# Hyena convolution at half-integer frequencies with an even/odd split, and a minimum in banded attention

## The reference

```python
def _bidir_long_conv(u, h_fwd, h_bwd, skip):
    l = u.shape[1]
    n = 2 * l
    filt = jnp.concatenate([h_fwd, jnp.zeros_like(h_fwd[:1]), h_bwd[:0:-1]], axis=0)
    uf = jnp.fft.rfft(u.astype(jnp.float32), n=n, axis=1)
    ff = jnp.fft.rfft(filt, n=n, axis=0)
    y = jnp.fft.irfft(uf * ff[None], n=n, axis=1)[:, :l]
    return (y + u.astype(jnp.float32) * skip.astype(jnp.float32)).astype(u.dtype)
```

## Time and profile before

| | |
|---|---|
| median of 3 runs | 2266.3 us (2265.16 to 2270.39) |
| profiled execution, its own time | 2263.19 us |
| its span, mean granted clock | 2261.4 us, 0.989 |
| busy: PE, PEld, DVE, ACT, POOL | 96%, 78%, 64%, 39%, 10% of the span |
| layer 1, last tile's end to w_out | 805.3 to 893.15 us from the span's start |
| layer 2, attention | 1394.8 to 1484.3 us |

### The profile page before, as it was taken

One profiled execution on the slowest core, in us unless ns is written; L12 is line 12 of the kernel. 1 busy time (PEld: TensorE's weight loads), 2 busy tenths in 40 slices (PEclk: granted clock), 3 DMA queues, 4 the chain that ended last, 5 costly groups with the idle time before them and its releaser, 6 DMA issues.

```text
span 2261.4 us, 28637 instructions
## 1 busy us (share of the span) xinstructions
PE 2161.1 (96%) x11616; PEld 1754.8 (78%) x11616; DVE 1439.3 (64%) x2224; ACT 885.7 (39%) x1337; POOL 216.7 (10%) x253
## 2 busy tenths in 40 slices
PE   6999999999999988999999999999999999998998
PEld 4767888888787756788888786478888878868996
DVE  3426668778666443658788745965778775655554
ACT  3335533332253411443332244845333223455543
POOL 0000011110010025011110002100111100100110
PEclk9999999999999989999999999999999999999999
DMA  9650345556532210335556522022455563214554
GB/s 312 201 172 1 112 130 168 158 158 205 205 119 74 84 37 10 112 112 161 165 157 215 195 86 84 2 84 94 148 168 159 189 202 126 94 38 140 187 186 140
DMA packets 224744, 304.96 MB, mean 135 GB/s; under 512 B 6738, under 2 KB 153243, under 8 KB 224486
## 3 DMA queue, kind: packets, MB, share of 16 engines
q1 hardware_dynamic: 220541, 290.11, 39.5%
q0 software_dynamic: 3664, 12.87, 1.7%
q10 hardware_dynamic: 409, 0.16, 0.0%
HBM read 302.00 MB, written 1.11 MB: 134 GB/s over the span
## 4 chain that ended last, share of the span: by engine, by line
PE 78%; DVE 11%; ACT 5%; DMA 4%; issue 2%; POOL 0%; SPq 0%; ACTq 0%; DVEq 0%; POOLq 0%
PE lo L648 16%; PE lo L650 16%; PE lo L649 16%; PE lo L714 4%; PE lo L715 3%; PE lo L716 3%; DVE w_lo L1471 2%; ACT w_hi L1126 2%; DMA w_raw<-in_ffn_w_down 2%; PE hi L714 2%; PE hi L715 2%; PE hi L716 2%; PE lo L1041 2%; PE hi L1054 1%; PE modp L614 1%
## 5 line engine op out<-in xcount | busy, mean ns | idle before, releaser
L648 PE MATMUL lo<-u_hi,w_hi 128*128 128x512 f32 (+1 forms) x2016 | 717.6, 356 | 5.5 <-DVE w_lo L1471 4.5
L649 PE MATMUL lo<-u_lo,w_hi 128*128 128x512 f32 (+1 forms) x2016 | 704.8, 350 | 0.0
L650 PE MATMUL lo<-u_hi,w_lo 128*128 128x512 f32 (+1 forms) x2016 | 704.3, 349 | 0.0
L1471 DVE TENSOR_TENSOR w_lo<-w_raw,w_hi 128x2048 fp32r<-128x2048 f32 (+1 forms) x182 | 406.7, 2235 | 343.1 <-ACT w_hi L1126 341.9
L1126 ACT ACTIVATE w_hi<-w_raw 128x2048 fp32r<-128x2048 f32 (+1 forms) x182 | 339.7, 1867 | 484.0 <-DMA w_raw<-in_ffn_w_down 262.5
L648 PEld LDWEIGHTS lo<-u_hi,w_hi 128*128 128x128 f32 x2016 | 382.5, 190 | 69.8 <-issue 17.5
L650 PEld LDWEIGHTS lo<-u_hi,w_lo 128*128 128x128 f32 x2016 | 382.4, 190 | 50.0
L649 PEld LDWEIGHTS lo<-u_lo,w_hi 128*128 128x128 f32 x2016 | 382.6, 190 | 49.1 <-issue 1.2
L1488 DVE SCALAR_TENSOR_TENSOR mod_acc<-mod_raw,silu_c,mod_acc 128x512 f32<-128x512 f32 x504 | 394.5, 848 | 7.3 <-DMA mod_raw<-in_mod_w 7.3
L2035 POOL TENSOR_TENSOR mid_lo<-conv,mid_hi 128x512 fp32r<-128x512 f32 (+1 forms) x88 | 117.8, 1358 | 1054.8 <-ACT mid_hi L1450 1054.8
L714 PE MATMUL lo<-w_hi,mid_hi 128*128 128x512 f32 x374 | 147.6, 395 | 4.9 <-DVE u_raw L1569 3.1
(11 more groups left out here) (314 smaller groups left out, 2741.6 us busy)
## 6 DMA issues: line engine op xcount, KB each, us to landing
w_raw<-in_ffn_w_up SPq DMA_DIRECT2D x88, 1024.0 KB, 5.1
mod_raw<-in_mod_w SPq DMA_DIRECT2D x144, 512.0 KB, 4.0
w_raw<-in_ffn_w_down SPq DMA_DIRECT2D x40, 1024.0 KB, 5.1
mod_unit<-in_mod_w SPq DMA_DIRECT2D x24, 1024.0 KB, 6.7
w_raw<-in_a_w_qkv SPq DMA_DIRECT2D x12, 1024.0 KB, 5.5
w_raw<-in_b_w_in SPq DMA_DIRECT2D x12, 1024.0 KB, 5.1
w_raw<-in_a_w_out SPq DMA_DIRECT2D x8, 1024.0 KB, 5.1
w_raw<-in_ffn_w_down SPq DMA_DIRECT2D x8, 512.0 KB, 3.6
```

The lines of the kernel that those rows point to most:

```text
L648: mm(o, h3[:, k, c], x, start=(first and k == 0), stop=False)
L649: mm(o, h3[:, k, c], y, start=False, stop=False)
L650: ins = mm(o, l3[:, k, c], x, start=False, stop=(last and k == nr - 1))
L1471: tt(WL[:, n % 3, 0:words], RAW[:, n % 3, 0:words], WH[:, n % 3, 0:words].bitcast(F32), ALU.subtract).then_inc(lo_ready, 1)
```

## The change

**Transform.** Frequencies k + 1/2 take the place of 0 to 256, so that no frequency is special and four blocks of filter_spec remain. Tokens are taken as 128 even and 128 odd ones (stationary operands with a step of two columns, rows of k_decay and k_dft reordered). For each of real and imaginary part one matmul on the even and one on the odd tokens (E and O) give frequency k as E + O and 255 - k as E - O (O - E for the imaginary part): ACT copies O out of PSUM (`odd_part`), DVE adds and subtracts (`butterflies`). A filter pair is two matmuls instead of four, a window's forward four instead of eight.

**Order.** Window 0 (turn, forward, butterflies, products, and POOL's y) and the turn of window 1 move into the tiles 8 to 11. `products` reads the spectrum from SBUF and writes two of its four products over it; y reads these. ACT makes both copies of a turn.

**Attention.** The fused operation of `peak` multiplies by -scale and takes the minimum, started from the negated sink; `negate` goes away for layer 2. `sinkn`, the negated sink, is made once; exp runs with scale -1.

```diff
+    pos = np.arange(SEQ, dtype=np.float64)[:, None]
+    th = 2 * np.pi * ((pos * (2 * np.arange(SEQ)[None, :] + 1)) % (2 * NFREQ)) / (2 * NFREQ)
+    out["k_dft"] = np.concatenate([np.cos(th[:, :P]), -np.sin(th[:, :P])], axis=1)[by_parity].astype(f)
+    order = np.concatenate([np.arange(P), SEQ - 1 - np.arange(P)])
+    ang = th.T[order]
+    out["k_idft"] = (2.0 / NFREQ * np.concatenate([np.cos(ang), -np.sin(ang)], axis=0)).astype(f)
...
         XFIRST = [FIRST["down" if k % 2 else "out", k // 2] for k in range(2 * DEPTH)]
+        def f_bank(w, j):
+            return bank[j + 4 if w == 0 else j]
+        def spectrum(w, j):
+            return XS[:, j, :] if w % 2 == 0 else (CV, SQ)[j % 2][:, j // 2, :]
         def x_bank(h, b):
...
                         ps = slice(FW * d, FW * d + FW)
-                        last = mm(bank[6 + d], FA[ps, 1, tt * P:(tt + 1) * P], W4[ps, hf * 512:(hf + 1) * 512],
+                        last = mm(bank[6 + d], FA[ps, 1, tt:SEQ:2], W4[ps, hf * 512:(hf + 1) * 512],
                                   start=True, stop=True)
                     last.then_inc(f_mm, 1)
                 else:
-                    pe.wait_ge(f_h, 4)
-                    for x in range(2 * (t - 7), 2 * (t - 7) + 2):
-                        j, hf = divmod(x, 2)
-                        if x >= 2:
-                            pe.wait_ge(f_sev, x - 1)
-                        src = HD if j in (2, 3) else HS
-                        blk = (0, 1, 5, 3, 4)[j]
-                        for kt in range(2):
-                            last = mm(bank[6 + x % 2], DF[:, kt, blk * P:(blk + 1) * P], src[:, kt, hf * 512:(hf + 1) * 512],
-                                      start=(kt == 0), stop=(kt == 1))
+                    for pair in ((0, 1), (2,), (3,), (), ())[t - 7]:
+                        hf, im = divmod(pair, 2)
+                        pe.wait_ge(f_h, 4)
+                        if pair >= 2:
+                            pe.wait_ge(f_sev, 2 if pair == 2 else 6)
+                        for e in range(2):
+                            last = mm(bank[(4 if pair == 1 else 6) + e], DF[:, e, im * P:(im + 1) * P],
+                                      (HD if im else HS)[:, e, hf * 512:(hf + 1) * 512], start=True, stop=True)
                         last.then_inc(f_spec, 1)
+            def turn_x1v(w):
+                hf, st = divmod(w, 2)
+                pe.wait_ge(z_conv, 2 * KT if hf == 0 else 3 * KT)
+                if w == 0:
+                    pe.wait_ge(f_sev, 4)
+                else:
+                    pe.wait_ge(c_vt, 2 * w)
+                if w == 1:
+                    pe.wait_ge(c_fly, 2)
+                for e in range(2):
+                    for c in range(4):
+                        last = nc.tensor.transpose(bank[4 + e][:, c * P:(c + 1) * P],
+                                                   XV[:, 4 * hf + c, st * SEQ + e:(st + 1) * SEQ:2], ident)
+                    last.then_inc(c_turned, 1)
+            def forward(w, im):
+                pe.wait_ge(c_vt, 2 * w + 2)
+                if w == 0 and im:
+                    pe.wait_ge(f_sev, 8)
+                if w == 1 and not im:
+                    pe.wait_ge(*released(PAIR0["in", 1] + 10))
+                if w == 1 and im:
+                    pe.wait_ge(z_evac, 3 * KT)
+                if w >= 2:
+                    pe.wait_ge(c_fly, 4 * w - 2 + 2 * im)
+                for e in range(2):
+                    last = mm(f_bank(w, 2 * im + e), DF[:, e, im * P:(im + 1) * P], VX[:, w % 2, e, :], start=True, stop=True)
+                last.then_inc(c_fwd, 1)
             def long_conv():
...
                 def inverse(w):
                     pe.wait_ge(c_y, 4 * (w + 1))
                     if w == 0:
                         pe.wait_ge(tab_in, TAB_AT[1] + 16)
...
                     else:
                         pe.wait_ge(c_skip, 4 * w)
...
+                def spectra(w):
+                    forward(w, 0)
+                    forward(w, 1)
+                spectra(1)
+                inverse(0)
+                turn_x1v(2)
+                spectra(2)
+                turn_x1v(3)
+                inverse(1)
+                spectra(3)
+                inverse(2)
+                inverse(3)
...
                         tile(n0 + t, q0 + t, TOK, UH, UL, True, True)
                         filter_stage(t)
+                        if t == 8:
+                            turn_x1v(0)
+                        if t == 9:
+                            forward(0, 0)
+                        if t == 10:
+                            forward(0, 1)
+                            turn_x1v(1)
                     long_conv()
                     arrive = lambda k: pe.wait_ge(c_lo, 8 * (k // 4 + 1))
-                    free = lambda b: ((c_prod, 32),)
+                    free = lambda b: ((c_fly, 16),)
                 else:
...
@@ -1267,7 +1282,7 @@
                     if A:
                         src, dst, sc = s_bank(x), p[:, 0:TOK], q_scale[:, 0, 4 * h + t:4 * h + t + 1]
                     else:
-                        src, dst, sc = p[:, 0:TOK + 1], p[:, 0:TOK + 1], 1.0
+                        src, dst, sc = p[:, 0:TOK + 1], p[:, 0:TOK + 1], -1.0
                     last = f(dst, src, ACT.Exp, scale=sc, bias=sl[:, 1, 0:1], accum_out=sl[:, 2, 0:1])
...
                         w = FW if t < 2 else 2 * FW
                         f(FA[0:w, (t + 1) % 2, :], FT[0:w, 0, :], ACT.Sin).then_inc(f_sin, 1)
-                    elif t >= 7:
-                        for x in range(2 * (t - 7), 2 * (t - 7) + 2):
-                            j, hf = divmod(x, 2)
-                            act.wait_ge(f_spec, x + 1)
-                            f(BF[:, j, hf * 512:(hf + 1) * 512], bank[6 + x % 2], ACT.Copy).then_inc(f_sev, 1)
+                    for pair in {7: (0, 1), 8: (2,), 9: (3,)}.get(t, ()):
+                        hf, im = divmod(pair, 2)
+                        act.wait_ge(f_spec, pair + 1)
+                        f(BF[:, 2 * im + 1, hf * 512:(hf + 1) * 512], bank[(4 if pair == 1 else 6) + 1], ACT.Copy).then_inc(f_odd, 1)
+                    if t in (9, 10):
+                        odd_part(0, t - 9)
+                    if t in (8, 10):
+                        turned((t - 8) // 2)
+            def odd_part(w, im):
+                act.wait_ge(c_fwd, 2 * w + im + 1)
+                if w >= 2:
+                    act.wait_ge(c_y, 4 * (w - 1))
+                f(spectrum(w, 2 * im + 1), f_bank(w, 2 * im + 1), ACT.Copy).then_inc(c_odd, 1)
+            def turned(w):
+                for e in range(2):
+                    act.wait_ge(c_turned, 2 * w + e + 1)
+                    if w >= 2:
+                        act.wait_ge(c_fwd, 2 * w - 2)
+                    f(VX[:, w % 2, e, :], bank[4 + e], ACT.Copy).then_inc(c_vt, 1)
             def long_conv():
-                def vt(w):
-                    act.wait_ge(c_turned, w + 1)
-                    if w >= 2:
-                        act.wait_ge(c_fwd, w - 1)
-                    f(VX[:, w % 2, 0, :], bank[4], ACT.Copy).then_inc(c_vt_act, 1)
                 def part(w):
                     hf, st = divmod(w, 2)
...
                     if t == 0:
                         dve.wait_ge(*((tab_in, TAB_AT[i]) if i else (start_in, 32)))
+                    if t + i == 0:
+                        ts(sinkn[:, :], sinkb[:, :], -1.0, None, ALU.mult)
                     for j in turned_in(i, t + 1):
                         rope(i, j)
...
@@ -1715,8 +1745,8 @@
                     w = TOK // nb
                     for b in range(nb):
                         ins = nc.vector.tensor_tensor_reduce(PB[:, x % 6, b * (CTX + 4):b * (CTX + 4) + w],
-                                                             s_bank(x)[:, b * CTX:b * CTX + w], maskT[:, t % 2, TOK - w:TOK], scale,
-                                                             -3e38, ALU.add, ALU.max, sl[:, 0, b:b + 1])
+                                                             s_bank(x)[:, b * CTX:b * CTX + w], maskT[:, t % 2, TOK - w:TOK], -scale,
+                                                             sinkn[:, h:h + 1], ALU.add, ALU.min, sl[:, 1, b:b + 1])
                     return ins
                 def negate(x):
@@ -1724,11 +1754,7 @@
                     h, t = HALVES[i][x]
                     sl = small[:, x % 6, :, :]
                     nb = 1 if t < 2 else 2
-                    if A:
-                        ins = tt(sl[:, 1, 0:nb], sl[:, 0, 0:nb], q_scale[:, 1, 4 * h + t:4 * h + t + nb], ALU.mult)
-                    else:
-                        ins = ts(sl[:, 1, 0:nb], sl[:, 0, 0:nb], sinkb[:, h:h + 1], -1.0, ALU.max, ALU.mult)
-                    ins.then_inc(s_max, 1)
+                    tt(sl[:, 1, 0:nb], sl[:, 0, 0:nb], q_scale[:, 1, 4 * h + t:4 * h + t + nb], ALU.mult).then_inc(s_max, 1)
                 def normalise(x):
...
@@ -1826,36 +1854,45 @@
```

(88 more changed lines are left out.)

65 lines of the change are left out of this document (8 added, 57 removed).

## The result

The changed kernel takes 2229.54 us (median of three; 2228.43 to 2231.85), the kernel before 2265.73 us beside it: a ratio of 0.9839, 95% interval 0.9824 to 0.9854. A fourth execution, of 7484.71 us, was disturbed and is left out (with it the median would be 2230.69). The profiled execution took 2229.54 us, its span 2227.7 at a clock of 0.990: 33.7 us less span than before.

A forecast was written before the change was run, and what follows sets the result against it. TensorE carries 78% of the chain, with waits for POOL and DVE after the tiles. The Hyena layer's -27.8 us and attention's -4.3 sum to -32.1, giving 2234 us, range 2216 to 2245.

The forecast's parts named there:

- Tiles: Hyena input tiles: 13.7 us of filter matmuls removed, 12.7 us of work added; last tile ends 1.0 us earlier.
- Products and POOL exclude each other: After the tiles: products with two SBUF inputs and POOL run in turn, 15 us per window against 11.5 of TensorE.
- y(1): POOL's y of window 1 after the tiles: ends at 825.5 us; inverse(1) waits about 4 us for it.
- Waits before inverse(2) and inverse(3): TensorE behind the tiles waits some 5 and 7 us for y(2) and y(3), released by POOL.
- Strided operands at nothing: Every second column of x1*v and the sine layer as stationary operand: costs 0, upper bound 5 us.
- Attention: Banded attention: TensorE becomes the bound once its 0.18 us gap per pair closes, 24 pairs, -4.3 us; bounds -12 and 0.
- (a): Rival, after the tiles: products and POOL do overlap, w_out starts near 848.5, total 2217 us; chance 0.12.
- (b): Rival: attention gains nothing and strided loads cost 5 us, total 2243 us; chance 0.08.
- (c): Rival, last tile to w_out: TensorE stays at 1.2 GHz from its first wait, total 2272 us; chance 0.03.

The follow-up runs named there:

- spectra in PSUM: Changed kernel with butterflies of windows 1 to 3 writing to PSUM, so each product has one input there; 2221.82 us, ratio 0.9802.
- second profile: The changed kernel run again with no edit to it; 2231.52 us, ratio 0.9848.
- the minimum alone: Kernel before with only the minimum in banded attention changed, Hyena layer untouched; 2263.74 us against 2266.46, ratio 0.9989.
- w_lo later: Changed kernel with DVE forming w_lo of the second w_out tile behind skip(2) instead of in tile 11; 2226.4 us, ratio 0.9831.
- The transform alone: Changed kernel with the maximum and small DVE operation put back in attention; 2236.18 us, ratio 0.9864.
- window 0 behind the tiles: Changed kernel with turn(0), forward(0), products(0) and the turn of window 1 after the last input tile; 2243.54 us, ratio 0.9891.

## Why the prediction was right, and where it was not

The forecast was 2234 us in the median and -32.1 us in the sum; measured were 2229.5 us and -33.7 us of span. The main mechanism, products and POOL in turn, is the one that the runs show; the reason given for attention is not. By its steps:

- **Tiles.** -1.0 forecast, -1.5 measured. The counts of matmuls carried it, and no wait appeared there. The other 0.5 us is the price of a turn: the prediction took 0.60 us for four transposes, the length of a record, but a group begins 0.44 us before the next (863.90 and 864.34 in the kernel before; 0.46 after), and four groups stand in the tiles.
- **Products and POOL exclude each other.** Right, and the spectra in PSUM show that the two SBUF inputs are the cause. The term was mis-sized by a little: "in turn that is 15 us" is 14.0. In strict turn an alternating pair would take 0.60 + 1.23 = 1.83 us and is 1.67 (821.22 - 819.54 = 1.68); beside a 256-column operation 0.60 + 0.69 = 1.29, and is 1.13. So 0.16 us of each pair is hidden, and one window has eight products. The Trainium skill (SBUF — State Buffer, "SBUF: two separate sides") says that the one that starts first gets the ports for the whole instruction and the other "fully blocks"; read as strict turns, an estimate, that gives 1.83. The main part agrees, and the measurement decides on the 0.16.
- **y(1).** Forecast 21.3 us after the tile's end, measured 20.4. The wait before inverse(1) was 3.0 instead of 4.
- **Waits before inverse(2) and inverse(3).** 5 and 7 forecast, 3.4 and 5.1 measured (1.7 and 6.8 in the second profile), released by y as said. The forecast had no slow clock in inverse(1) and inverse(2); in each of the four profiles one of them has it, and it only moves wait from one place to the other. Two windows of 14 instead of 15 are 2 us of the 3.4 by which w_out came earlier, counted from the tile's end, than forecast; the rest is y(1)'s 0.9 and 0.5 at inverse(3), which took 9.4 us for 6.9 + 3.0.
- **Strided operands at nothing.** Right: a filter-layer matmul with every second column takes 644 ns in the median of 16 records (641 before) and a group of four transposes begins 0.46 us before the next (0.44 before).
- **Attention.** -4.3 forecast, -4.0 measured, and -5.0 where no stretch ran at the lower clock (86.2 to 81.2 in the minimum alone). The size was right by luck, and the reason given for it, "TensorE is the bound", was wrong. Two errors met. The new form is 0.06 us dearer, 3.8 us in all, where the sum had no such term (it stood only as a bound). And what DVE saved net, 12 - 3.8 = 8.2 us, came through to some 60%, with more to be had: taking the reciprocal away brought another 3.6 us. The step that failed is the reading of 0.18 us of visible gap as all that TensorE lost. Its busy time is no measure of that, as the counts of 249, 261 and 280 show. What sets the pace now is open. In these 40 us DVE waits 3.2 us for scores from TensorE with the reciprocal and 5.9 without it, and ACT is busy for 36.2 without it; the engines wait for each other in turn, and no run separates them.
- **Rivals.** (a), overlap, is out by the stretched rows. No run reached its 2217 us: with the spectra in PSUM in windows 1 to 3 the time is 2221.8, with w_lo later too 2219.4. (b) is out: attention gained and strided loads cost nothing. (c) is out: the clock came back each time, and the three inverses after waits took 0, 1.7 and 2.3 us more than 7.1.
- **Luck.** The stages sum to -35.6 us, 3.5 more than forecast. The +2.4 us ahead of the layer, which no term of the forecast has and whose cause is open, brings the profiled span back to within 1.6 us of it.

## What to carry to other kernels

Before moving an input of a DVE operation from PSUM to SBUF, look at what POOL does at that time: the operation may stay at 0.6 us alone and still hold POOL up by 0.45 us each time. Keeping an intermediate in PSUM in place was worth more here than freeing the bank early (7.4 us, with the new wait of 3.8 us already paid). And where an engine reads as busy for the whole stretch, count its instructions per microsecond before calling it the bound. Where waits shift from one profile to the next, compare the start of the last piece of work behind them.

## What was not expected

- DVE and POOL in alternation are cheaper than strict turns: 1.67 us for 1.83 (512 columns both), 1.13 for 1.29 (512 beside 256).
- A minimum with its start value from a buffer costs 0.06 us more than one with a constant: 746 ns for 686 at 512 columns, 480 for 421 at 256, a fixed cost.
- A single late DVE operation cost twice: w_lo, 2.29 us alone, took 3.36 (it begins beside POOL's last addition but one) and stretched POOL's last addition from 1.26 to 3.31.
- Attention of the changed kernel shows a stretch of 0.83 granted clock (1370 to 1380 us) that the kernel before, the minimum alone, both kernels with spectra in PSUM and the one with w_lo later don't have; it goes with the 1.0 us between 82.2 and 81.2. It appeared in both profiles of the changed kernel and without the reciprocal. The transform alone and window 0 behind the tiles have longer ones (88.7 and 84.2 us of attention), which is 2 us of what the latter lost. What brings it was not tried.
